# First mixer: VectorE's convolution taps summed in PSUM, two channel groups for each engine, and the layer norm's wide passes on GpSimd

## The reference, cut to what matters

```python
def conformer_conv(u, conv_w, conv_b, ln_g, ln_b):
    a, g = jnp.split(u, 2, axis=-1)
    h = a * jax.nn.sigmoid(g)
    h = jnp.pad(h, ((0, 0), (CONV_KERNEL - 1, 0), (0, 0)))      # CONV_KERNEL = 31
    y = lax.conv_general_dilated(h, conv_w[:, None, :], ..., feature_group_count=CONV_WIDTH)
    y = y + conv_b
    return jax.nn.silu(layer_norm(y, ln_g, ln_b))               # over the 512 channels
...
hid = jax.nn.gelu(einsum('bnkf,fh->bnkh', blocks, w1))          # compressed keys and values
k_cmp = einsum('bnkh,hd->bnkd', hid, w2)
...
mixed = jnp.concatenate([attn_out, conv_out], axis=-1)
x = x + jnp.einsum('bsm,md->bsd', mixed, w_out[layer])
```

## Time and profile before

| | us |
|---|---|
| median of 3 runs | 3132.37 |
| lowest and highest | 3129.27, 3139.49 |
| the profiled execution's own time | 3140.26 |
| its span, first to last instruction | 3138.4 |

### The profile page before, as it was taken

The page is one execution under the profiler, slowest core; times in us unless marked ns, Lnnn a source line. Parts: engine busy times, 40 slices in busy tenths (PEclk is TensorE's granted clock), DMA queues, the critical chain, the costliest instruction groups (busy, mean ns, idle before and its releaser), DMA issues.

```text
span 3138.4 us, 34504 instructions
## 1 busy us (share of the span) xinstructions
PE 2972.0 (95%) x15102; PEld 1779.2 (57%) x15102; DVE 837.4 (27%) x1689; ACT 408.6 (13%) x1045; POOL 180.3 (6%) x249
## 2 busy tenths in 40 slices
PE   7699999779999999999997999999999999999998
PEld 5457777444333333333333776576776776576776
DVE  4735453741000000100011333242332002142002
ACT  4520002531000000000001001131001001131000
POOL 6300003400000000000000000000000000000000
PEclk9889999889999999999998999999999999999999
DMA  6139884315999999999996764414764444413442
GB/s 217 68 124 319 294 308 144 126 54 207 381 369 389 358 368 383 368 373 380 369 379 221 255 222 150 150 58 159 253 219 147 146 144 151 157 54 134 142 146 94
DMA packets 266287, 704.57 MB, mean 224 GB/s; under 512 B 9286, under 2 KB 132439, under 8 KB 241556
## 3 DMA queue, kind: packets, MB, share of 16 engines
q1 hardware_dynamic: 225072, 622.39, 54.3%
q10 hardware_dynamic: 38036, 75.61, 6.8%
q0 software_dynamic: 3024, 4.31, 0.5%
HBM read 698.07 MB, written 1.05 MB: 223 GB/s over the span
## 4 chain that ended last, share of the span: by engine, by line
PE 87%; DVE 7%; DMA 2%; ACT 2%; issue 1%; POOL 0%; DVEq 0%; SPq 0%; ACTq 0%; POOLq 0%
PE PS L1762 84%; DMA ring<-in_moe_w_up_dram 2%; DVE M L1262 1%; DMA ring<-in_w_in_dram 1%; PE PS L2141 1%; PE PS L1973 0%; DVE SM L1645 0%; DVE SM L1389 0%; ACT R L1000 0%; PE PS L1788 0%; ACT R L681 0%; PE PS L2349 0%; DVE SM L1067 0%; DVE SM L1065 0%; DVE PS L1642 0%
## 5 line engine op out<-in xcount | busy, mean ns | idle before, releaser
L1762 PE MATMUL PS<-XT,ring 128*128 128x256 f32 x4480 | 1005.0, 383 | 11.7 <-ACT GS L980 8.0
L1762 PEld LDWEIGHTS PS<-XT,ring 128*128 128x128 f32 x4480 | 858.3, 192 | 178.6 <-issue 55.8
L1762 PE MATMUL PS<-ring,R 128*32 128x256 f32 (+2 forms) x3616 | 720.1, 490 | 0.6 <-ACT R L889 0.6
L1762 PEld LDWEIGHTS PS<-ring,R 128*32 128x32 f32 (+2 forms) x3616 | 291.6, 137 | 368.5 <-issue 331.9
L1762 PE MATMUL PS<-ring,GS 128*64 128x384 f32 (+4 forms) x2176 | 305.3, 527 | 2.5 <-DMA ring<-in_moe_w_up_dram 1.7
L1762 PE MATMUL PS<-ring,KZ 128*64 128x512 f32 (+3 forms) x2048 | 301.9, 543 | 1.3 <-DMA ring<-in_moe_w_up_dram 1.3
L1147 DVE TENSOR_TENSOR QT<-QT,PS 128x256 f32<-128x256 f32 x116 | 48.9, 421 | 827.9 <-ACT QT L740 827.9
L1762 PEld LDWEIGHTS PS<-ring,GS 128*32 128x32 f32 (+1 forms) x2176 | 103.3, 122 | 199.3 <-issue 192.0
L1762 PEld LDWEIGHTS PS<-ring,KZ 128*64 128x64 f32 (+1 forms) x2048 | 99.5, 123 | 197.7 <-issue 190.8
L1762 PE MATMUL PS<-ring,XT 128*128 128x512 f32 (+2 forms) x512 | 199.6, 552 | 1.2 <-ACT XT L704 1.2
L740 ACT ACTIVATE QT<-PS 128x256 f32<-128x256 f32 x116 | 44.6, 384 | 1091.8 <-PE PS L1762 1091.8
(11 more groups left out here) (322 smaller groups left out, 1690.0 us busy)
## 6 DMA issues: line engine op xcount, KB each, us to landing
ring<-in_moe_w_gate_dram SPq DMA_DIRECT2D x32, 2048.0 KB, 11.1
ring<-in_moe_w_up_dram SPq DMA_DIRECT2D x32, 2048.0 KB, 11.2
ring<-in_moe_w_down_dram SPq DMA_DIRECT2D x32, 2048.0 KB, 10.9
ring<-in_moe_w_gate_dram SPq DMA_DIRECT2D x32, 1536.0 KB, 11.5
ring<-in_moe_w_up_dram SPq DMA_DIRECT2D x32, 1536.0 KB, 7.1
ring<-in_moe_w_down_dram SPq DMA_DIRECT2D x32, 1536.0 KB, 8.6
ring<-in_ffn_wg_dram SPq DMA_DIRECT2D x44, 1024.0 KB, 5.4
ring<-in_ffn_wu_dram SPq DMA_DIRECT2D x44, 1024.0 KB, 7.9
```

The lines of the kernel that those rows point to most:

```text
L1762: return e.matmul(o, lhsT, rhs, start=first, stop=last)
```

## The change

1. VectorE takes all 31 taps of groups 2 and 3 (62 instead of 46), and their running sums are no longer in `Y` but in PSUM, the two halves of bank 2 (`YP`). Of the 62, 10 stay before `glue(3)` and 52 come after it: 1 first one, 41 that alternate with the other group, and the last 10 of group 3 in a row. ScalarE copies `YP` to `Y` once (128x512), after the squares of block 0.
2. ScalarE and GpSimd keep groups 0 and 1: 62 products instead of 78, 60 adds instead of 75, and the sum `YB` with its last add is gone. ScalarE's last taps now lie between the projection's copies; none is left behind them.
3. The mean's matmul moves on TensorE from i = 2 to a place ahead of the query transposes, into bank 0, and the mean's copy on ScalarE ahead of the `QT` copies; `scores(0)` waits for that copy.
4. The subtraction of the mean and the product with the reciprocal root (each 128x1024) go from VectorE to GpSimd, at the end of its queue. The root (`rsqrt`) moves from i = 6 to i = 5, the squares from i = 3 to i = 1, the variance's matmul from i = 4 to i = 5.
5. The gelu's sigmoid goes on ScalarE between the copies of the two key groups, and the gelu's last product on VectorE behind `soft(0)`. The compressed keys' matmul moves from i = 4 to i = 1, `compressed()` from i = 5 to i = 3, their transposes from i = 6 to i = 4, `compressed_turned()` from i = 7 to i = 4, with new places in PSUM banks 3 and 6.

```diff
-        OWN = [(k, 2) for k in range(10)] + [t for k in range(15) for t in ((k, 3), (k + 10, 2))]
-        OWN += [(k, 2) for k in range(25, 31)]
+        OWN = [(k, 2) for k in range(10)] + [t for k in range(21) for t in ((k, 3), (k + 10, 2))]
+        OWN += [(k, 3) for k in range(21, 31)]
...
-        TAPS += [t for k in range(15, 31) for t in ((k, 1), (k, 3))]
+        TAPS += [(k, 1) for k in range(15, 31)]
...
+        YP = PS[:, 2, :].rearrange("p (c n) -> p c n", c=2)
...
 # gpsimd
-                e.tensor_tensor(Y[:, 3, :], Y[:, 3, :], YB, ADD).then_inc(s_cadd.sem, 1)
+                e.wait_ge(*s_lnc(st, 1))
+                e.tensor_tensor(Y[:, :, :], Y[:, :, :], bc(MEAN, [P, 4, 256], (1,)), SUB).then_inc(s_lns.sem, 1)
+                e.wait_ge(*s_lns(st, 1))
+                e.wait_ge(*s_lnt(st, 1))
+                e.tensor_tensor(Y[:, :, :], Y[:, :, :], bc(RS2, [P, 4, 256], (1,)), MUL).then_inc(s_lnn.sem, 1)
 # scalar
-                    if n % 2:
-                        if n > 1:
-                            squared(n // 2 - 1)
-                        taps((8, 4, 0)[n // 2])
+                    if n % 2 == 0:
+                        taps(8)
+                    elif n == 1:
+                        taps(4)
                     else:
-                        taps(8)
+                        squared(n // 2 - 1)
+                    if n == 3:
+                        e.wait_ge(*s_own(st, 2))
+                        e.activation(Y[:, 2:4, :], YP, ACT.Copy).then_inc(s_ycp.sem, 1)
+                        taps(4)
...
+                e.wait_ge(*s_lnm(st, 1))
+                e.activation(MEAN, PS[:, 0, 0:256], ACT.Copy, scale=1.0 / 512).then_inc(s_lnc.sem, 1)
...
-                    taps(6)
-                assert len(done) == len(TAPS)
-                e.wait_ge(*s_gelu(st, 1))
-                e.activation(HB[:, 62:124], ...ACT.Sigmoid...)
+                    if k == 0:
+                        e.wait_ge(*s_gelu(st, 1))
+                        e.activation(HB[:, 62:124], ...ACT.Sigmoid...)
 # vector
-                            t = e.scalar_tensor_tensor(out=Y[:, ch, :], in0=h, scalar=w, in1=Y[:, ch, :], op0=MUL, op1=ADD)
+                            t = e.scalar_tensor_tensor(out=y, in0=h, scalar=w, in1=y, op0=MUL, op1=ADD)   # y = YP[:, ch - 2, :]
...
-                taps(36)
+                taps(52)
...
+                    if i == 0:
+                        e.wait_ge(*s_gels(st, 1))
+                        e.tensor_tensor(u_gel, x, u_gel, MUL).then_inc(s_gel.sem, 1)
                     if i == 3:
-                        e.wait_ge(*s_lnc(st, 1))
-                        e.tensor_tensor(Y[:, :, :], Y[:, :, :], bc(MEAN, [P, 4, 256], (1,)), SUB).then_inc(s_lns.sem, 1)
+                        compressed()
+                    if i == 4:
+                        compressed_turned()
                     if i == 5:
                         e.wait_ge(*s_lnv(st, 1))
                         e.tensor_scalar(RS, PS[:, 6, 0:256], 1.0 / 512, EPS, MUL, ADD).then_inc(s_lnr.sem, 1)
-                        compressed()
-                    if i == 6:
                         e.wait_ge(*s_lnr(st, 1))
-                        rsqrt(RS2, RS, RS3)
-                        e.wait_ge(*v.last())
-                        e.tensor_tensor(Y[:, :, :], Y[:, :, :], bc(RS2, [P, 4, 256], (1,)), MUL).then_inc(s_lnn.sem, 1)
-                    if i == 7:
-                        compressed_turned()
+                        rsqrt(RS2, RS, RS3, s_lnt)
 # tensor, behind the compressed blocks' matmuls and ahead of the query transposes
+                e.wait_ge(*s_cadd(st, 60))
+                e.wait_ge(*s_ycp(st, 1))
+                for ch in range(4):
+                    w = mm(PS[:, 0, 0:256], ones, Y[:, ch, :], ch == 0, ch == 3)
+                w.then_inc(s_lnm.sem, 1)
...
```

More of the change, by code:

```diff
@@ L322, in build @@
         s_kc = signal("s_kc", mix1=1)
-        s_y0 = signal("s_y0", mix1=3)
-        s_ct = signal("s_ct", mix1=75)
-        s_cadd = signal("s_cadd", mix1=76)
+        s_y0 = signal("s_y0", mix1=2)
+        s_ct = signal("s_ct", mix1=60)
+        s_cadd = signal("s_cadd", mix1=60)
+        s_ycp = signal("s_ycp", mix1=1)
         s_rot = signal("s_rot", mix1=2)
@@ L797, in mix1 @@
                     projected(n)
[L798 to L803 removed]
+                    if n % 2 == 0:
+                        taps(8)
+                    elif n == 1:
+                        taps(4)
+                    else:
+                        squared(n // 2 - 1)
[3 more added lines that the diff above has]
+                        taps(4)
+                assert len(done) == len(TAPS)
                 e.activation(GT, PRB[:, :, 1280:1304], ACT.Sigmoid).then_inc(s_gt.sem, 1)
                 e.wait_ge(*s_hp(st, 1))
[L806 to L807 removed]
+                e.activation(HIDS, PS[:, 3, 0:256], ACT.Copy).then_inc(s_hids.sem, 1)
+                e.wait_ge(*s_lnm(st, 1))
+                e.activation(MEAN, PS[:, 0, 0:256], ACT.Copy, scale=1.0 / 512).then_inc(s_lnc.sem, 1)
                 for b in range(2):
@@ L1062, in rsqrt @@
                 e.tensor_scalar(x, x, -0.5, None, MUL).then_inc(*v.up())
-                for _ in range(3):
+                for i in range(3):
                     e.wait_ge(*v.last())
@@ L1068, in rsqrt @@
                     e.wait_ge(*v.last())
-                    e.scalar_tensor_tensor(out=y, in0=t, scalar=1.5, in1=y, op0=ADD, op1=MUL).then_inc(*v.up())
+                    w = e.scalar_tensor_tensor(out=y, in0=t, scalar=1.5, in1=y, op0=ADD, op1=MUL)
+                    if sig and i == 2:
+                        w.then_inc(sig.sem, 1)
+                    else:
+                        w.then_inc(*v.up())
             def norm(k, b):
@@ L2008, in mix1 @@
                         turn_p(i - 2)
-                    if i == 2:
-                        e.wait_ge(*s_cadd(st, 76))
-                        e.wait_ge(*s_own(st, 2))
-                        e.wait_ge(*s_k(st, 8))
-                        for ch in range(4):
-                            w = mm(PS[:, 6, 0:256], ones, Y[:, ch, :], ch == 0, ch == 3)
-                        w.then_inc(s_lnm.sem, 1)
                     if i >= 3:
                         values(i - 3)
-                    if i == 4:
+                    if i == 1:
+                        e.wait_ge(*s_gel(st, 1))
+                        e.wait_ge(*s_k(st, 4))
+                        for q in range(2):
+                            for u in range(2):
+                                w = mm(PS[0:NCMP, 6, 128 * q + u * 64:128 * q + u * 64 + 64],
+                                       HB[:, 62 + 32 * q + u * 15:77 + 32 * q + u * 15], W2[:, 2 * l + q, :], True, True)
+                        w.then_inc(s_kc.sem, 1)
+                    if i == 4:
+                        e.wait_ge(*s_kcs(st, 1))
+                        e.transpose(PS[:, 6, 256:256 + NCMP], KC15[0:NCMP, :], ident[0:NCMP, 0:NCMP])
+                        e.transpose(PS[:, 6, 272:272 + NCMP], HB[0:NCMP, 0:128], ident[0:NCMP, 0:NCMP]).then_inc(s_kcT.sem, 1)
+                    if i == 5:
+                        e.wait_ge(*s_kcz(st, 1))
                         e.wait_ge(*s_lnq(st, 1))
@@ L2022, in mix1 @@
                         w.then_inc(s_lnv.sem, 1)
-                        e.wait_ge(*s_gel(st, 1))
-                        e.wait_ge(*s_ex(st, 4))
-                        for q in range(2):
-                            for u in range(2):
-                                w = mm(PS[0:NCMP, 2, 128 * q + u * 64:128 * q + u * 64 + 64],
-                                       HB[:, 62 + 32 * q + u * 15:77 + 32 * q + u * 15], W2[:, 2 * l + q, :], True, True)
-                        w.then_inc(s_kc.sem, 1)
-                    if i == 6:
-                        e.wait_ge(*s_kcs(st, 1))
-                        e.transpose(PS[:, 3, 0:NCMP], KC15[0:NCMP, :], ident[0:NCMP, 0:NCMP])
-                        e.transpose(PS[:, 3, 16:16 + NCMP], HB[0:NCMP, 0:128], ident[0:NCMP, 0:NCMP]).then_inc(s_kcT.sem, 1)
                     if i == 9:
```

58 lines of the change are left out of this document (25 added, 33 removed).

## The result

The changed kernel takes 3120.39 us (median of 8 runs, 3115.19 to 3121.51), the kernel before 3132.83 (8 runs, 3129.27 to 3139.49): ratio 0.9953, 95% interval 0.9942 to 0.9965. It is faster by about half a per cent. The profiled execution took 3116.34 us, its span is 3114.5.

What follows compares the result with a forecast made beforehand. TensorE, 87% of the chain, bounds the kernel; gains lie where it waits in the mixers' relay, carried longest by VectorE. First layer -7.5 and second -12.4 make -19.9, from a median of 3132.4 to 3112.5 us; range 3100 to 3130.

Steps and rivals of the forecast that it cites:

- the forecast's own range: Whole kernel: the case that the forecast holds, 3104 to 3120 us, chance 0.60.
- rival B: Score steps: VectorE's freed passes return as waits, so these steps give nothing; 3123 us, from 3120 to 3132, chance 0.20.
- The taps: VectorE's taps, summed in PSUM at 0.476 us each, run unhindered by GpSimd: second layer -6.5 us, first +4.9.
- Rival A: Taps at L1262 still share with GpSimd, 41 to 46 us for the 52; about 3145 us, slower side, chance 0.12.
- The prediction's own argument against it: PSUM mask: 0.69 us for 512 columns, 0.53 streaming, leaves 0.16, said not to bear out the dearer PSUM source.
- The head norms: Up to head norm 1's end, with 2.3 us charged for GpSimd's subtraction: second layer -4.2 us, first +0.2.
- Gelu, last taps, mean: First scores to `soft(3)`: the gelu's and the mean's gains together, -4.7 us in the first layer, -5.2 in the second.
- The gelu's term: Key copies to first exponential: 12 taps, sigmoid and product no longer hold up `soft(0)`; -3.0 us first layer, -3.5 second.
- The mean's term: TensorE between the first transposes and `scores(3)`: the mean's matmul leaves, -1.7 us in each layer.
- rival C: More than forecast: subtraction falls between operations, product blocks nothing, TensorE's matmuls at `scores(2)` run at high clock; -30, 3102 us, chance 0.08.
- Score steps: `soft(3)` to `scores(8)`: two VectorE passes go and `compressed()` fills idle time, -5.0 less waits, so -3.0 us each layer.
- The warning sign: Score steps: the prediction is wrong if VectorE shows new idle time at i = 4 or 5 of more than 3 us.

Runs made afterwards that it cites:

- the repetition: The changed kernel run once more, unaltered: 3117.61 us, ratio 0.9947 to the kernel before.
- sbuf_taps: The changed kernel with the running sums of VectorE's taps in SBUF instead of PSUM, ScalarE's copy left out: 3133.11 us, ratio 0.9992 to the kernel before.
- taps_only: The kernel before with parts 1 and 2 of the change alone, everything from the mean on as before: 3119.86 us, ratio 0.9954 to the kernel before.
- variance_early: The changed kernel with the variance's matmul at i = 5 right behind the scores, ahead of transposes and values product: 3113.4 us, ratio 0.9928 to the kernel before.
- root6: The changed kernel with the variance's scale and the root moved back from i = 5 to i = 6 on VectorE: 3120.42 us, ratio 0.9948 to the kernel before.
- gelu_before_scores: The changed kernel with the sigmoid behind both key copy groups and its product ahead of the first softmax step: 3119.52 us, ratio 0.9947 to the kernel before.

## Why the prediction was right, and where it was not

The forecast was 3112.5 us, a gain of 19.9; the medians gave 12.4, the ratio 0.9953 some 14.7 (11.0 to 18.2), the repetition 0.9947 some 16. Both times lie in the range, and faster by over 0.3% was the likeliest case. The repetition lies in the forecast's own range of 3104 to 3120; the first median, 3120.39, lies just outside it, where rival B begins. The runs show a mixture of the two: the gains up to `soft(3)` came as forecast or better, and in the score steps rival B's case came true.

*The taps* (-6.5, +4.9): right. 0.476 was taken for a tap, 0.481 and 0.485 measured, 21.3 us for 51 instead of some 21.4; with the first one the stretch of the first layer grew by 4.6 us. The last tap of the second layer ends 6.7 us earlier in its stage. Rival A did not come true, the reading of the earlier trace rows held, and sbuf_taps shows that the place of the sum, and not the dealing, is what parts the engines. This agrees with the Trainium skill (SBUF — State Buffer, section "SBUF: two separate sides"), by which VectorE takes the shared ports in a two-port mode or with two SBUF inputs. Here one tensor input of a tap lies in PSUM, and neither a tap nor an add is held up, although the weight of each channel still comes from SBUF. The dearer PSUM source that the Trainium skill has (VectorE: DVE Perf Modes, section "The TRN2 errata"), by estimate 65 ns a tap, does not show: the medians with sums in PSUM and in SBUF are 481 and 480 ns. The prediction's own argument against it was weak, since the 0.16 us that it had left over could hold such a cost; these two medians decide it. Its reading of the 9585 ns add was too narrow as well: a single tap lasts 0.476 us, so that add stood behind a whole run of them.

*The head norms*: right in the second layer (-4.2; end of head norm 1 -4.2, first scores -3.6), 2 us too dear in the first (+0.2; -1.8, first scores -2.4). There the compressed blocks' sums took 5.9 us (83.1 to 89.0) instead of the 8 taken from the earlier trace rows: with adds no longer starved they run at the second layer's pace. The subtraction itself, estimated at 2.3, took 2.34 and 3.08, and the stall behind it 2.1 and 2.0 (2.50 and 2.38 less 0.36).

*Gelu, last taps, mean* (-4.7, -5.2): -5.4 and -6.2, near, but by another split. The gelu's term (-3.0, -3.5), read from the first scores to the first exponential, is -2.8 and -2.3 (6.8 to 4.0 us, 7.4 to 5.1); in the second layer the first scores ran at a clock of 0.77 and took 1.1 us more than before. The 12 taps make this term, the gelu's new place adds nothing. The mean's term (-1.7), read from there to `soft(3)`, is -2.6 and -3.9, and of it 1.2 and 1.8 are the clock in the third score group (3.18 and 3.78 to 1.99), which rival C spoke of: TensorE idle for less long ahead of `scores(2)`. That part came with the taps alone, for in taps_only this group takes 1.99 us too. What lies between taps_only (14.2 / 14.2) and the whole change is 0.8 and 0.7 us, net of the first two score groups (5.64 and 5.76 there, 3.69 and 4.78 here). So the mean's move itself was worth about half of its 1.7, and the clock, which the sum did not have, made up for it: luck.

*Score steps* (-3.0, -3.0): **the term that failed.** Measured +0.1 and -0.1: rival B's place. The sum had "the root at i = 5 waits for the variance matmul, which TensorE reaches 1 us later than VectorE does"; VectorE waited 4.2 and 4.0 us, for TensorE does the transposes and the values product of the step first, and then the matmul, all at a low clock (0.58 and 0.60 on average over the three), which the sum had priced at 1 us, without the clock. In the second layer the account closes: -2.3 for the two passes, -2.7 for the old wait that `compressed()` filled, +4.0 for the new one, +0.9 behind GpSimd's product, together -0.1. The warning sign was named, new idle time at i = 4 or 5 of more than 3 us, and it was there. variance_early shows the cause: with the matmul two places earlier the stretch falls by 3.2 and 3.6 us, more than the forecast's 3.0. No run parts the order from the clock; the estimate above gives the clock some 2.5 of the 4.0 us. root6 shows that moving the root alone mostly moves the wait. The other suspect, the product on GpSimd, cost 0.9 us once (626.63, 1.05 instead of 0.17), near the 1.0 taken.

*The chances* do not quite add up as stated: slower was given 0.13, though only rival A holds it, with 0.12 and its mild end counted as same. No reading hangs on it.

Left open: the time up to the scores varies between kernels that are the same there. In the first layer the taps begin at 61.9 in the changed kernel and at 63.95 in taps_only. The late start comes from TensorE's input projection (first the changed kernel, then taps_only):

```profile
29.46 24.44 PE L1769 MATMUL PS<-XT,ring 128*128 128x256 f32 x112 [1.26 <-DMA ring<-in_w_in_dram]
...
29.83 26.13 PE L1759 MATMUL PS<-XT,ring 128*128 128x256 f32 x112 [2.00 <-DMA ring<-in_w_in_dram]
```

A longer wait for the weights, and behind it a granted clock of 0.83 instead of 1.00 from 30 to 40 us; gelu_before_scores shows the same (2.43 us and 0.83). Likewise the transposes between head norm 1 and the first scores take 3.9, 5.4 or 6.0 us, and the first score groups 3.69 in one profile and up to 5.76 in another. What decides the clock at these places was not tried, so no difference under 2 us in these stretches is read by itself, unless a single operation of the trace carries it.

## What to carry to other kernels

Where VectorE and GpSimd both work on SBUF, first ask which operand can live in PSUM: one operand moved there gave both engines their full pace, and nearly the whole gain. When an operation is moved to an idle engine, price what runs beside it: each wide pass made its neighbour on VectorE 0.9 to 2.1 us longer wherever it ran, but behind the norms, for one added wait, that neighbour was one that the scores do not wait for. And before counting a gain in a relay, look at when the last input of the moved step is made, on the producer's own queue, and at which clock: the order of a few things on TensorE decided whether 3 us a layer were kept.

## What the runs showed of the hardware that was not expected

A GpSimd operation is not only slow beside VectorE operations on SBUF, it can stand still behind a run of them: one add of 0.73 us lasted 14.7 us in sbuf_taps, while 0.48 us taps ran back to back, yet in the second layer of the same kernel the two mostly took turns, a tap at 0.83 to 0.95 us. In both kernels with the sums in SBUF the add stood still where the taps had begun first (61.7 and 61.5, the first add at 64.3 and 64.1), and they took turns where adds were already running; whether this is what decides was not tried. It goes the other way too: one VectorE operation of 0.36 us took 2.38 and 2.50 beside a 128x1024 pass of GpSimd. In variance_early it fell on one of 0.96 us, which took 2.98, again 2.0 more:

```profile
576.08 2.98 DVE L1249 TENSOR_TENSOR R<-R,G 128x768 f32<-128x768 f32 x1
```

The same 16 score matmuls took 3.69, 4.78, 5.00 or 5.76 us, at mean granted clocks of 1.00, 0.77, 0.74 and 0.64, which is as much as most single steps of this change are worth.
